# A two-layer decoder trunk: VectorE makes the low parts around the first quarter, and the expert selection is rewritten

## The reference, cut to what matters

```python
h = h + concat[FoX | NSA | Diff heads] @ W_out
h = h + PEER(rmsnorm(h))
h = h + sigmoid(rmsnorm(h) @ W_g) * (p @ W_p)

def peer_ffn(x, w_q, sub_keys, u, v):       # 8 heads, 128 x 128 experts of one neuron
    q = (x @ w_q).reshape(b, s, 8, 2, 128)
    sc = einsum('bshcd,hcnd->bshcn', q, sub_keys)
    s1, i1 = top_k(sc[..., 0, :], 16)
    s2, i2 = top_k(sc[..., 1, :], 16)
    cand = s1[..., :, None] + s2[..., None, :]          # 256 sums per token and head
    top_s, pos = top_k(cand, 16)
    eidx = i1[pos // 16] * 128 + i2[pos % 16]
    gate = softmax(top_s)
    hid = gelu(einsum('btd,bthkd->bthk', x, u[eidx]))
    return einsum('bthk,bthkd->btd', gate * hid, v[eidx])
```

## Time and profile before

| | |
|---|---|
| median of 3 runs | 2394.24 us |
| profiled execution | 2381.31 us, span 2379.3 us |
| busy in the span | TensorE 92%, VectorE 74%, ScalarE 39%, GpSimd 46% |
| mean granted clock of TensorE | 0.966 of full speed |
| transfers | 342.53 MB, 144 GB/s over the span |

### The profile page before, as it was taken

The page is one execution under the profiler, slowest core; times in us unless marked ns, Lnnn a source line. Parts: engine busy times, 40 slices in busy tenths (PEclk is TensorE's granted clock), DMA queues, the critical chain, the costliest instruction groups (busy, mean ns, idle before and its releaser), DMA issues.

```text
span 2379.3 us, 46392 instructions
## 1 busy us (share of the span) xinstructions
PE 2190.4 (92%) x18032; PEld 1965.9 (83%) x18032; DVE 1761.1 (74%) x2571; ACT 930.0 (39%) x1305; POOL 1088.7 (46%) x450
## 2 busy tenths in 40 slices
PE   4899997788999999999887999977899999999997
PEld 4777897667989999999877788976679998999996
DVE  2545389999988888677436445899999879886773
ACT  3434443333444434443434334432334443443433
POOL 3722577333444444444556235873334444444444
PEclk9999999799999999999988999997999999999999
DMA  4411343233454444555433113532344444545552
GB/s 181 161 36 55 127 168 130 83 133 139 177 176 169 168 175 176 177 183 187 146 120 125 36 72 125 173 123 78 141 142 176 176 167 169 176 171 182 185 185 89
DMA packets 47700, 342.53 MB, mean 144 GB/s; under 512 B 5488, under 2 KB 5488, under 8 KB 6384
## 3 DMA queue, kind: packets, MB, share of 16 engines
q1 hardware_dynamic: 46896, 336.89, 39.8%
q10 hardware_dynamic: 704, 4.26, 0.5%
HBM read 340.08 MB, written 1.05 MB: 143 GB/s over the span
## 4 chain that ended last, share of the span: by engine, by line
PE 72%; DVE 23%; ACT 2%; issue 2%; DMA 0%; DVEq 0%; SPq 0%; ACTq 0%
PE psum L415 20%; PE psum L416 20%; PE psum L417 20%; DVE arena L1415 3%; DVE wl L348 3%; PE psum L652 3%; DVE arena L1411 2%; PE psum L429 2%; DVE arena L1427 2%; DVE arena L1328 1%; DVE arena L1325 1%; PE psum L581 1%; DVE arena L1410 1%; PE psum L537 1%; PE psum L564 1%
## 5 line engine op out<-in xcount | busy, mean ns | idle before, releaser
L348 POOL TENSOR_TENSOR wl<-ring,wh 128x1024 fp32r<-128x1024 f32 (+1 forms) x404 | 1039.7, 2594 | 1152.1 <-ACT wh L341 1152.1
L341 ACT ACTIVATE wh<-ring 128x1024 fp32r<-128x1024 f32 x628 | 625.6, 1046 | 459.3 <-PE psum L417 459.3
L415 PE MATMUL psum<-xh,wh 128*128 128x256 f32 (+1 forms) x2320 | 665.0, 287 | 8.5 <-POOL wl L348 7.9
L416 PE MATMUL psum<-xl,wh 128*128 128x256 f32 (+1 forms) x2320 | 656.6, 283 | 0.0
L417 PE MATMUL psum<-xh,wl 128*128 128x256 f32 (+1 forms) x2320 | 656.5, 283 | 0.0
L415 PEld LDWEIGHTS psum<-xh,wh 128*128 128x128 f32 (+1 forms) x2320 | 443.5, 191 | 15.1 <-POOL wl L348 6.4
L415 PE MATMUL psum<-wh,Wh 128*128 128x512 f32 (+1 forms) x1056 | 415.1, 393 | 40.7 <-DVE Wl L1439 38.7
L416 PEld LDWEIGHTS psum<-xl,wh 128*128 128x128 f32 (+1 forms) x2320 | 443.8, 191 | 1.3
L417 PEld LDWEIGHTS psum<-xh,wl 128*128 128x128 f32 (+1 forms) x2320 | 443.6, 191 | 0.2
L416 PE MATMUL psum<-wl,Wh 128*128 128x512 f32 (+1 forms) x1056 | 410.7, 389 | 0.0
L417 PE MATMUL psum<-wh,Wl 128*128 128x512 f32 (+1 forms) x1056 | 409.5, 388 | 0.0
(11 more groups left out here) (221 smaller groups left out, 2408.3 us busy)
## 6 DMA issues: line engine op xcount, KB each, us to landing
ring<-stream SPq DMA_DIRECT2D x318, 1024.0 KB, 4.8
arena<-keys ACTq DMA_DIRECT2D x2, 1024.0 KB, 6.1
smr<-rows SPq DMA_DIRECT2D x1, 1090.0 KB, 11.3
smr<-rows ACTq DMA_DIRECT2D x1, 1090.0 KB, 5.1
h<-x SPq DMA_DIRECT2D x1, 1024.0 KB, 5.3
out<-h ACTq DMA_DIRECT2D x1, 1024.0 KB, 4.1
sm<-cols SPq DMA_DIRECT2D x1, 728.0 KB, 9.3
kst<-consts SPq DMA_DIRECT2D x1, 495.0 KB, 7.9
```

What stands on the lines that cost most here:

```text
L341: nc.scalar.activation(wh[:, buffer_of(L, n), c], ring[:, (L * SLOTS + n) % RING, c], ACT.Copy).then_inc(hi_ok, 1)
L348: eng.tensor_tensor(wl[:, b, c], ring[:, (L * SLOTS + n) % RING, c], wh[:, b, c].bitcast(F32), ALU.subtract).then_inc(done, 1)
L415: pe.matmul(o, a[0], b[0], start=start, stop=False, **kw)
L416: pe.matmul(o, a[0], b[1], start=False, stop=False, **kw)
```

## The change

- **Low parts.** GpSimd makes those of `u` slots 0 to 7 (`EARLY = 8`), VectorE those of `u` slots 8 to 16 (`low_lead`, semaphore `ulo_ok`) and both halves of the 16 `v` slots of the first quarter. After that it is as before.
- **First products.** TensorE does 0 to 8 in the selection, 9 after the ranks, and 10 to 16 after blocks 3, 5, ... 15.
- **Second selection over 80 sums.** Of the 16 x 16 sums five groups of 16 are made (`STAIR`): rank 0 with all 16, rank 1 with all 16, ranks 2 and 3 with the first 8, 4 to 7 with the first 4, 8 to 15 with the first 2. Other sums cannot be among the 16 largest. Shifts and an exclusive-or get the two ranks out of a position.
- **Rank sums on TensorE.** VectorE compares and multiplies, with the rank as the outer dimension; the 16 products are then added and turned by 64 matmuls with an identity. Fold, reduction and four of the six transposes are gone.
- **Gate table key by key.** ScalarE evicts a block so that a key's 256 tokens lie side by side, and `weigh` reads in order. GELU's output of the first 17 pairs is laid down in the same order (`lead_slot`).
- **Start and end.** The angle tables come after the first norm. In the last part each chunk's addition follows its multiplication, and in layer 1 SyncE sends each chunk out.

```diff
+STAIR = 5
+CANDS = STAIR * TOPK
+EARLY = 8
+U_DVE = [u_slot(p) for p in range(EARLY, LEAD)]
+REST = [n for n in SPLIT if n not in V_ALL and n not in U_DVE]
+        prod = ar(A_EQ, T * PH * TOPK * TOPK).bitcast(BF16).rearrange("p (c r n) -> p c r n", c=2, r=TOPK)
+        def lead_slot(p):
+            return ar(A_LEAD, QI, SEQ)[:, :, bass.ds(p * TB, TB)]
 ...
 # SyncE, at the end
+            for i in range(N_PLEG):
+                sp.wait_ge(part_ok, i + 1)
+                c = slice(i * CHUNK, (i + 1) * CHUNK)
+                sp.dma_start(rows_out[:, :, c], h[:, :, c]).then_inc(out_st, 16)
 ...
 # TensorE
-                for k in range(1, 4):
-                    hidden(0, k, 4)
-                with pe.Fori(1, QP // 4 - 1) as i:
-                    for k in range(4):
-                        hidden(i, k, 4)
-                hidden(0, QP - 4)
+                for p in range(1, EARLY + 1):
+                    hidden(0, p)
 ...
+                pe.wait_ge(prod_ok, L + 1)
+                for c in range(2):
+                    for t in range(T):
+                        for r in range(TOPK):
+                            pe.matmul(bank(6, P, at=c * SEQ + t * P), prod[:, c, r, t * P:(t + 1) * P], identb[:, :],
+                                      start=(r == 0), stop=(r == TOPK - 1))
                 pe.wait_ge(rout_ok, L + 1)
-                for k in range(3):
-                    for t in range(T):
-                        ins = pe.transpose(bank(6 + k // 2, P, at=(k % 2) * SEQ + t * P), rout[:, k, t, :], ident)
+                for t in range(T):
+                    ins = pe.transpose(bank(7, P, at=t * P), rout[:, t, :], ident)
-                hidden(0, QP - 3)
+                hidden(0, EARLY + 1)
                 for n in range(NB):
                     spread(q0 + n, n % 2, n)
-                    if n in (1, 3, 5):
-                        hidden(0, QP - 2 + n // 2)
+                    if n % 2 and n > 1:
+                        hidden(0, EARLY + 1 + n // 2)
 ...
 # ScalarE, gates_out
-                    buf = ar((quarter % 2) * SEQ * QI, SEQ * QI)
-                    act.activation(buf[:, bass.ds((step * i + n) * TB * QI, TB * QI)], bank(6 + n % 2, 512),
+                    buf = ar((quarter % 2) * SEQ * QI, QI, SEQ)
+                    act.activation(buf[:, :, bass.ds((step * i + n) * TB, TB)],
+                                   bank(6 + n % 2, TB, QI).rearrange("p t e -> p e t"),
                                    ACT.Copy, scale=1.0 / G_SCALE).then_inc(g_ok, 1)
 ...
 # GpSimd
-                with pool.Fori(0, QP // 4 - 1) as i:
-                    for k in range(4):
-                        low(L, u_slot(k), i)
-                for p in range(QP - 4, QP + 1):
+                for p in range(EARLY):
                     low(L, u_slot(p))
-                with pool.Fori(0, QP // 4) as i:
-                    for k in range(4):
-                        low_half(pool, L, v_slot(k), i, 1, vlo2_ok)
 ...
 # VectorE
+                def low_lead(p):
+                    for j in range(2):
+                        low_half(dve, L, u_slot(p), 0, j, ulo_ok)
 ...
+                for k in range(STAIR):
+                    rows_, width = max(1, 1 << k >> 1), TOPK >> max(0, k - 1)
+                    a = first[:, :, 0:1] if k == 0 else first[:, :, rows_:2 * rows_]
+                    out_ = flat[:, :, k * TOPK:(k + 1) * TOPK].rearrange("p n (a b) -> p n a b", b=width)
+                    step(dve.tensor_tensor(out_, last(a, width), mid(second[:, :, 0:width], 2, rows_), ALU.add))
 ...
+                low_lead(EARLY)
 ...
+                low_lead(EARLY + 1)
 ...
-                    for j in range(1 if p < QP else 2):
+                    for j in range(2):
                         low_half(dve, L, v_slot(p), i, j, vlo_ok)
                 for n in range(NB):
                     onehots(0, 0, n, first=(L == 0 and n < 2))
+                    if n % 2 and n < NB - 1:
+                        low_lead(EARLY + 2 + n // 2)
```

More of the change, by code:

```diff
@@ L1109, in _ @@
+            for L in range(LAYERS):
+                if L == 0:
+                    dve.wait_ge(ld_x, 16)
+                    dve.wait_ge(ld_cols, 16)
                 mean_rstd(L, 0)
+                if L == 0:
+                    tables()
                 def projected(chunks):
@@ L1339, in _ @@
                     best16([v16[:, t, j, :] for j in m], [i16[:, t, j, :] for j in m], [sc[:, t, j, :] for j in m])
-                for t in range(T):
-                    c4 = cand[:, t, :, :].rearrange("p h (a b) -> p h a b", a=TOPK)
-                    vv = v16[:, t, :, :].rearrange("p (h c) k -> p h c k", c=2)
-                    step(dve.tensor_tensor(c4, last(vv[:, :, 0, :], TOPK), mid(vv[:, :, 1, :], 2, TOPK), ALU.add))
+                first, second = (v16.rearrange("p t (h c) k -> p (t h) c k", c=2)[:, :, c, :] for c in range(2))
+                flat = cand.rearrange("p t h n -> p (t h) n")
+                n_ = T * PH
+                for k in range(STAIR):
[3 more added lines that the diff above has]
+                    step(dve.tensor_tensor(out_, last(a, width), mid(second[:, :, 0:width], 2, rows_), ALU.add))
                 settle()
@@ L1355, in _ @@
+                step(dve.tensor_scalar(shift, pos_, 4, 7, ALU.logical_shift_right, ALU.bitwise_xor))
+                step(dve.tensor_scalar(scaled, pos_, 15, 16, ALU.bitwise_and, ALU.bitwise_or))
+                for c in range(2):
+                    step(dve.tensor_copy(i16b[:, c].rearrange("p t r h -> p t h r"),
+                                         i16.rearrange("p t (h c) k -> p t h c k", c=2)[:, :, :, c, :]))
                 settle()
                 dve.tensor_tensor(c16, c16, last(gden[:, 0, :, :], TOPK), ALU.subtract).then_inc(ge_in, 1)
-                step(dve.tensor_copy(ranks2, last(ab16.rearrange("p c t n -> p c (t n)"), 2)))
+                step(dve.tensor_scalar(scaled, scaled, 2, None, ALU.logical_shift_left))
@@ L1369, in _ @@
-                    ii = i16b.rearrange("p (m c r) -> p m c r", c=2, r=TOPK)[:, :, c, :]
-                    step(dve.tensor_tensor(e4, e4, mid(ii, 2, TOPK), ALU.mult))
+                    step(dve.tensor_copy(ranks[:, c].rearrange("p (t k h) -> p t h k", t=T, k=TOPK),
+                                         ab16[:, c].rearrange("p (t h k) -> p t h k", t=T, h=PH)))
+                settle()
+                n2 = T * PH * TOPK // 2
+                for c in range(2):
+                    step(dve.tensor_tensor(prod[:, c].rearrange("p r (a b) -> p r a b", b=2),
+                                           mid(ranks[:, c].rearrange("p (a b) -> p a b", b=2), 1, TOPK),
+                                           mid(iota16[:, :, :], 2, n2), ALU.is_equal))
@@ L1371, in _ @@
+                low_lead(EARLY)
                 settle()
                 for c in range(2):
-                    e3 = eq[c].rearrange("p (n r) -> p n r", r=TOPK)
-                    step(dve.tensor_tensor(fold[c], e3[:, :, 0:8], e3[:, :, 8:16], ALU.add))
-                settle()
-                for c in range(2):
-                    step(dve.tensor_reduce(rout[:, c, :, :].rearrange("p t n -> p (t n)"), fold[c], AX, ALU.add))
+                    for t in range(T):
+                        e4 = prod[:, c, :, t * P:(t + 1) * P].rearrange("p r (k h) -> p r k h", h=PH)
+                        ins = dve.tensor_tensor(e4, e4, mid(i16b[:, c, t], 2, TOPK), ALU.mult)
```

172 lines of the change are left out of this document (90 added, 82 removed).

## The result

The changed kernel takes 2303.3 us (median of four executions), the kernel before on the same chip 2394.1 (2391.5 to 2394.4). The other three take 2300.8, 2300.8 and 2305.8, and the ratio is 0.962 (95% interval 0.960 to 0.964). The prediction was 2326 with a range of 2308 to 2352: faster as said, but 23 us too dear, and outside the range.

A forecast was written before the change was run, and what follows sets the result against it. TensorE bounds most of the kernel but waits 45 us a layer for VectorE. Gains 55.4 (two layers) + 5.1 + 3.6 + 3.7 = 67.8 took the profiled 2381.3 to 2313.5; plus 12.9, 2326; range 2308 to 2352.

The forecast's parts named there:

- the last step: End of the sum: 12.9 us, median over profiled execution of the kernel before, added to 2313.5, giving 2326.
- First quarter, 6.6 us a pair: Sixteen second products of the first quarter: TensorE becomes the bound, 105.6 us for 123.8, gain 18.2 a layer.
- Step 2: Stretch until the first second product: ends at 454.6 us for 464.1, gain 9.5 a layer.
- Sums: VectorE before the second selection: five instructions of 256 numbers, 1.5 us alone, 5.9 if two meet GpSimd; 3.7 taken.
- the index math: Ranks out of positions on VectorE: 14 small instructions, 3.5 us alone, four held up by GpSimd; 13 taken, bounds 4 and 17.
- The wait before product 8: TensorE, first products done at about 365, waits 9 us for VectorE's low part of slot 8.
- The idle at blocks 0 to 3: TensorE, doing product 9 and three gate blocks under VectorE's one-hots and low part, idles about 7 us.
- Start 5.1, change of layer 3.6, end 3.7: Gains in us: tables after the first norm; three additions under matmuls between layers; additions covered and smaller last transfer at end.
- rivals 2 and 5: ScalarE's turned eviction in the first quarter is slow: 2344 us (chance 0.10), or slower than before, 2416 at x = 7 (0.03).
- rival 1: VectorE's 16-bit work, equality tests or multiplications, is slower than thought or waits more on GpSimd: 2342 us; chance 0.15.
- rival 3: First quarter: the 2.2 us are not GpSimd's, so a pair costs 8.4 and the time is 2384 us; chance 0.05.
- rival 4: The 64 rank matmuls cost 15 us, 512 columns' price each: 2348 us; chance 0.05.

## Why the prediction was wrong

The miss is 2326 against 2303.3. I split it as 7.8 us of terms (2313.5 for a profiled execution, 2305.75 came) and 15 us of the last step, which went from the profiled execution to the median. Without that step the forecast would have been 2313.5 and the range 2295 to 2339, which holds the result.

- **"The median of the runs is 2394.2, 12.9 above; I take the same difference from it."** This step failed. The 12.9 is no fixed offset: the kernel before spans 20 us in step with TensorE's granted clock, and small products in the attention loop brought that to 3.2. The changed kernel's own median lay 2.5 below its profile, not 12.9 above. Why all four executions of before on the first chip lay at the long end and those of the changed kernel did not, the runs don't say. With the clock held the change is worth 79.4, where the prediction's terms give 67.8. So the terms were 11.6 short, and the 90.8 between the medians also hold a difference of clock.
- **First quarter, 6.6 us a pair: right** (6.55), and its reason is shown: one half back on GpSimd costs 0.7 us a pair. The margin was thinner than 6.3 against 6.55 said; without the key-by-key table VectorE needs 6.8.
- **Step 2, 9.5 a layer: right in what waits, wrong in size** (13.6). Selection 16 (16.05), equality 4.4 (4.5) and 64 matmuls 3.8 (3.74) came as said. Sums took 6.25 for 3.7, since two of the five met GpSimd, my upper end. The mis-sized term is the index math: 13 taken, 8.4 measured, because GpSimd was done at 360.2 and held up one instruction, not four. (The copy just before that one took 0.74 as well, where it takes 0.17 in the run with 256 sums.) The wait before product 8 was 6.1 for 9. The idle at blocks 0 to 3 was 5.4 for 7; the prediction's own terms (386 to 399.8, less 5.85 and 3 x 0.95) give 5.1, so its 7 was a slip that its sum does not use.
- **Start 5.1, change of layer 3.6, end 3.7: right** (5.0, 3.5 and about 3.5; 12.1 for all three when undone).
- **Rivals.** The turned eviction costs nothing (0.60 us, rivals 2 and 5), VectorE's 16-bit work came as priced (rival 1), the 2.2 us are GpSimd's (rival 3), the rank matmuls cost 3.7 (rival 4). The range had no case in it for the time of before being at one end of its own scatter.

The Trainium skill, "SBUF — State Buffer", Who interferes with whom, says that the ports are locked for a whole instruction. The multiplication that takes 2.89 us for 0.68 beside a GpSimd half agrees. The same section exempts a VectorE instruction with at most one input in SBUF, outside the modes that use both pairs of ports. The prediction used only the first of these two statements; the selection's MAX8, which has one input and takes 0.87 to 0.88 us with and without GpSimd (last section), agrees with the second.

## What to carry to other kernels

Look at several executions and their mean granted clock before carrying a difference over; three equal times can all be at one end, and a gain of 3 to 4% is then off by half a per cent. Where VectorE is the bound, a 2.4 us piece handed to GpSimd costs VectorE 2.2 us if it catches a multiplication, subtraction, addition or scaling like those here, nearly twice what doing it itself costs (1.2); hand it over only beside work that is not held up. And where an engine idles in the middle of a list of covered work, ask which instruction of the engine it waits for could go first, before giving that work to a third.

## What the runs showed that I had not expected

GpSimd does not hold up the selection. Four MAX8 of the first selection take as long while GpSimd runs (320.78 and 329.31) as while it rests (327.22); VectorE's and GpSimd's timelines in the changed kernel:

```profile
320.78 0.88 DVE L1348 MAX8 arena<-arena 128x8 f32<-128x128 f32 x4
...
327.22 0.87 DVE L1348 MAX8 arena<-arena 128x8 f32<-128x128 f32 x4
...
329.31 0.87 DVE L1348 MAX8 arena<-arena 128x8 f32<-128x128 f32 x4
```

```profile
317.86 4.76 POOL L357 TENSOR_TENSOR wl<-ring,wh 128x1024 fp32r<-128x1024 f32 x2 [2.79 <-ACT wh L350]
327.74 9.68 POOL L357 TENSOR_TENSOR wl<-ring,wh 128x1024 fp32r<-128x1024 f32 x4 [5.12 <-ACT wh L350]
```

FIND_INDEX8 and MATCH_REPLACE8 take 0.27 to 0.29 us in both cases too. Right behind the selection, single instructions of the sums (2.62) and of the index math (2.49, for 0.28 of the same form just before) are held up by some 2.2 us. So a low part of GpSimd was free beside the selection, and cost VectorE some 2 us where it met such an instruction.

The other is the clock: a loop in which TensorE's records show almost no idle was granted half the clock for 10 to 24 us in one layer of a profile and not in the other, and with 0.2 us of small products per unit the end of the loop was at full clock in every profile. Why it falls is open.
